# Rows of the routed tokens by one-hot products in every expert turn

## What is computed

```python
def _hier_moe(u, p, l):
    g_idx = jnp.argmax(g_logits, axis=-1)                  # one group of 4
    top_v, top_i = lax.top_k(e_in, TOP_K)                  # 2 experts of its 4
    w = jax.nn.softmax(top_v, axis=-1) * p_group[..., None]
    ...
    hg = jnp.einsum('bld,edf->blef', u, p['moe_w_gate'][l])
    hu = jnp.einsum('bld,edf->blef', u, p['moe_w_up'][l])
    h = jax.nn.silu(hg) * hu * gates.astype(u.dtype)[..., None]
    return jnp.einsum('blef,efd->bld', h, p['moe_w_down'][l])
```

## Time and profile before

| | us |
|---|---|
| median of 3 runs (1232.44 to 1235.7) | 1234.98 |
| the profiled execution | 1224.85 |
| its span | 1223.0 |
| TensorE busy, matmuls | 1114.9 (91%) |
| TensorE busy, weight loads (beside the matmuls) | 622.1 (51%) |
| VectorE busy | 389.9 (32%) |
| ScalarE busy | 233.9 (19%) |
| POOL busy | 140.8 (12%) |

### The profile page before, as it was taken

How to read it: one execution, slowest core, us unless ns; L and a number is a source line. 1 busy time by engine, 2 the same in 40 slices (tenths; PEclk the granted TensorE clock), 3 DMA queues, 4 the chain that set the end, 5 groups by cost and what they waited for, 6 DMA issues and landing times.

```text
span 1223.0 us, 23538 instructions
## 1 busy us (share of the span) xinstructions
PE 1114.9 (91%) x10201; PEld 622.1 (51%) x10201; DVE 389.9 (32%) x1023; ACT 233.9 (19%) x501; POOL 140.8 (12%) x163
## 2 busy tenths in 40 slices
PE   5899999899989959988889999999998995998986
PEld 3443445555575535545455555545666553555543
DVE  3201331574251300111233633587624230101104
ACT  2002201321231111101053232321012111111112
POOL 1043100022120000000010000042232000000001
PEclk9999999999989989999999999999998998999998
DMA  9998755359559998999996202002395999899994
GB/s 385 398 304 288 312 206 209 145 174 406 200 233 336 405 386 331 371 395 417 416 324 209 73 16 69 1 1 69 153 360 218 367 407 383 324 374 398 406 419 176
DMA packets 73018, 338.24 MB, mean 277 GB/s; under 512 B 6740, under 2 KB 16243, under 8 KB 58128
## 3 DMA queue, kind: packets, MB, share of 16 engines
q1 hardware_dynamic: 60760, 299.14, 63.2%
q0 software_dynamic: 10864, 36.42, 8.6%
q10 hardware_dynamic: 1288, 1.14, 0.3%
HBM read 314.24 MB, written 22.44 MB: 275 GB/s over the span
## 4 chain that ended last, share of the span: by engine, by line
PE 68%; DMA 18%; DVE 7%; issue 2%; ACT 2%; SPq 1%; POOL 1%; ACTq 0%; DVEq 0%; POOLq 0%
PE ps L2359 16%; DMA ring<-in_moe_w_up 12%; PE ps L1987 11%; PE ps L2562 10%; PE ps L2065 8%; PE ps L2383 7%; PE ps L2622 3%; DMA ring<-in_rec_w_in 3%; PE ps L2008 2%; PE ps L2292 2%; PE ps L2592 1%; PE ps L2342 1%; PE ps L2369 1%; PE ps L1980 1%; ACT work L1183 1%
## 5 line engine op out<-in xcount | busy, mean ns | idle before, releaser
L2359 PE MATMUL ps<-ring,work 128*32 128x256 f32 x4736 | 295.8, 394 | 53.4 <-DMA ring<-in_moe_w_up 49.3
L2359 PEld LDWEIGHTS ps<-ring,work 128*32 128x32 f32 x4736 | 150.4, 113 | 152.4 <-issue 66.3
L2562 PE MATMUL ps<-uT,ring 128*128 128x386 f32 x384 | 128.8, 488 | 0.9 <-issue 0.9
L2383 PE MATMUL ps<-ring,work 128*32 128x256 f32 x1728 | 103.0, 380 | 2.1 <-DVE work L1814 2.1
L2562 PEld LDWEIGHTS ps<-uT,ring 128*128 128x128 f32 x384 | 71.7, 190 | 49.6 <-issue 2.4
L1814 DVE COPY work<-ps 128x128 f32<-128x128 f32 x74 | 21.5, 291 | 235.4 <-PE ps L2369 234.3
L2065 PE MATMUL ps<-uT,ring 128*128 128x384 f32 x256 | 89.2, 505 | 3.0 <-DMA ring<-in_rec_w_in 1.9
L1195 ACT ACTIVATE work<-ps 128x128 f32<-128x128 f32 x74 | 20.5, 277 | 337.0 <-PE ps L2359 337.0
L1987 PE MATMUL ps<-ring,uT 128*128 128x512 f32 x192 | 84.1, 595 | 0.0
L2383 PEld LDWEIGHTS ps<-ring,work 128*32 128x32 f32 x1728 | 55.8, 110 | 39.8 <-DVE work L1814 3.0
L1810 DVE TENSOR_TENSOR work<-ps,work 128x128 f32<-128x128 f32 x74 | 21.6, 292 | 155.6 <-ACT work L1195 155.6
(11 more groups left out here) (371 smaller groups left out, 1194.9 us busy)
## 6 DMA issues: line engine op xcount, KB each, us to landing
ring<-in_moe_w_gate SPq DMA_DIRECT2D x32, 2048.0 KB, 12.8
ring<-in_moe_w_up SPq DMA_DIRECT2D x32, 2048.0 KB, 18.0
ring<-in_ada_w SPq DMA_DIRECT2D x24, 2048.0 KB, 11.3
ring<-in_moe_w_down SPq DMA_DIRECT2D x22, 2048.0 KB, 24.1
uT<-in_moe_w_down SPq DMA_DIRECT2D x10, 1536.0 KB, 16.4
ring<-in_rec_w_in SPq DMA_DIRECT2D x6, 2048.0 KB, 23.5
ring<-in_hy_w_in SPq DMA_DIRECT2D x6, 2048.0 KB, 13.4
y_rows<-work SPq DMA_DIRECT2D x64, 96.0 KB, 12.7
```

Source lines behind the costliest of these rows:

```text
L2359: ins = pe.matmul(bank(key)[32 * q:32 * q + 32, 0:2 * P].rearrange("p (a n) -> p a n", a=2), xg[:, u, k, 32 * i:32 * i + 32], ring[:, 3 * ...
L2383: ins = pe.matmul(bank(key)[32 * q:32 * q + 32, 0:256], hT[:, (FIRST[p] + i) % 2, 32 * k:32 * k + 32], w[:, q * 256:(q + 1) * 256], start= ...
L2562: ins = pe.matmul(bank(key)[:, 0:T + 2], w[:, k, (m % 4) * P:(m % 4 + 1) * P], uH[:, k, :], start=(k == 0), stop=(k == DC - 1))
```

## The change

The rows of all turns are now gathered as turn 0's were. `rows_t(p, h)` is 12 products a half (4 feature blocks by 3 token blocks) with the token rows as weights and `oh0[:, j, 0:n]` as what streams, n being 96, 64 or 32, where there were four transposes. It waits for the turn's table (`first_slots`). `fixed_slots` builds the tables of turns 0 to 2, `ranked_slots` those of the ranked turns, from the slot numbers that VectorE has: two small subtractions, three comparisons and three that compare and add. There is one buffer `oh0`, so each waits for the products of the turn before. POOL does not scatter or load rows any more; it stores the three blocks of `utok` to `x_rows` once, for the overflow path, which loads them back from there in plain order if it is taken. The clearing of `x_rows` is gone, and so is SyncE's wait for the rows. POOL's gather of results waits for the last turn's products, since it overwrites `utok`.

```diff
@@ SyncE, step(p)
                     full(sp, (l, p, "GU", TILES[p] - 1))
-                    if p == 0:
-                        sp.wait_ge(S("rows1_loaded"), 16 * (l * (NE // 2) + 1))
-                        sp.wait_ge(S("rows0_loaded"), 16 * (l * (NE // 2 - 1) + 1))
                     load_part(0, e, u)
@@ POOL
-            for a0, p_, n in ((0, P, ROWS // P), (ROWS // P * P, ROWS % P, 1)):
-                pool.dma_start(x_dram[a0:a0 + p_ * n, :].rearrange("(p a) (h n) -> p (a h) n", p=p_, n=512),
-                               bc(zeros[0:p_].unsqueeze(1), [p_, 2 * n, 512])).then_inc(S("x_rows_cleared"), 16)
...
-                pool.wait_ge(S("rows_known"), l + 1)
-                if l == 0:
-                    pool.wait_ge(S("x_rows_cleared"), 32)
                 for n, j in enumerate(BY_ROWS):
                     pool.wait_ge(S("u_rows"), NT * l + n + 1)
-                    for q in range(2):
-                        pool.indirect_dma_start(x_dram, bass.IndirectOffsetOnAxis(ap=ridx[:, j, q:q + 1], axis=0),
-                                                utok[:, j, :], None).then_inc(S("x_rows_stored"), 16)
-                pool.wait_ge(S("x_rows_stored"), 16 * 2 * NT * (l + 1))
-
-                for p in range(1, NE):
-                    u, n = p % 2, CAPS[p]
-                    if p >= 2:
-                        full(pool, (l, p - 2, "X", 1))
-                    pool.dma_start(ug[0:n, u, :], x_dram[BASES[p]:BASES[p] + n, :]).then_inc(S(f"rows{u}_loaded"), 16)
-
+                    pool.dma_start(x_dram[j * P:(j + 1) * P, :], utok[:, j, :]).then_inc(S("row_tables"), 16)
                 pool.wait_ge(S("picks_known"), l + 1)
                 for u in range(2):
                     pool.wait_ge(S(f"y{u}_stored"), 4 * 16 * STORED * (l + 1))
+                full(pool, (l, NE - 1, "X", 1))
@@ VectorE
-                for j in range(NT):
-                    ins = v.tensor_scalar(oh0[:, j, :], iota[:, 0:CAP], pl[:, j, 0:1], mask[:, j, 0:1], ALU.is_equal, ALU.mult)
-                ins.then_inc(S("first_slots"), 1)
+
+                def fixed_slots(p):
+                    if p:
+                        full(v, (l, p - 1, "X", 1))
+                    for j in range(NT):
+                        ins = v.tensor_scalar(oh0[:, j, :], iota[:, 0:CAP], pl[:, j, p:p + 1], mask[:, j, p:p + 1], ALU.is_equal, ALU.mult)
+                    ins.then_inc(S("first_slots"), 1)
+
+                def ranked_slots(p):
+                    n, local = CAPS[p], [R5[q][:, :, 0] for q in range(2)]
+                    full(v, (l, p - 1, "X", 1))
+                    v.tensor_scalar(local[0], R1[7], -float(BASES[p]), None, ALU.add)
+                    chain(v.tensor_scalar(local[1], R1[8], -float(BASES[p]), None, ALU.add))
+                    for j in range(NT):
+                        ins = v.tensor_scalar(oh0[:, j, 0:n], iota[:, 0:n], local[0][:, j:j + 1], None, ALU.is_equal)
+                    chain(ins)
+                    for j in range(NT):
+                        ins = v.scalar_tensor_tensor(oh0[:, j, 0:n], iota[:, 0:n], local[1][:, j:j + 1], oh0[:, j, 0:n], ALU.is_equal, ALU.add)
+                    ins.then_inc(S("first_slots"), 1)
+
+                fixed_slots(0)
...
                 ins.then_inc(S("rows_known"), 1)
+                fixed_slots(1)
...
                 rows_in(1)
+                fixed_slots(2)
...
                             rows_in(p + 1)
+                            if p + 2 < NE:
+                                ranked_slots(p + 2)
@@ TensorE, rows_t(p, h)
-                    if h == 0:
-                        pe.wait_ge(S(f"rows{u}_loaded"), 16 * (l * (NE // 2 - 1 + u) + p // 2 + u))
+                    pe.wait_ge(S("first_slots"), NE * l + p + 1)
                     opened(pe, key)
-                    for n in range(4):
-                        k = 4 * h + n
-                        ins = pe.transpose(bank(key)[:, n * CAP:n * CAP + n_], ug[0:n_, u, k * P:(k + 1) * P], ident[0:n_, 0:n_])
+                    for n, j in enumerate(BY_ROWS):
+                        for q in range(4):
+                            k = 4 * h + q
+                            ins = pe.matmul(bank(key)[:, q * CAP:q * CAP + n_], utok[:, j, k * P:(k + 1) * P], oh0[:, j, 0:n_],
+                                            start=(n == 0 and q == 0), stop=(n == NT - 1 and q == 3))
                     done(ins, key)
```

More of the change, by code:

```diff
@@ L75, in tables @@
         np.eye(P), (i[:, None] < i[None, :]), np.tile(i, (P, 1)),
-        i[:, None] + P * np.arange(NT)[None, :], np.tile([4, 3, 2, 1], (P, 1)),
+        i[:, None] + P * np.arange(NT)[None, :] - T, np.tile([4, 3, 2, 1], (P, 1)),
         np.tile(ROWS - CAP + P * np.arange(NE), (P, 1))], axis=1).astype(np.float32)
@@ L141, in build @@
         o = 3 * P
-        tokid, w4, obase = tc_[:, o:o + NT], tc_[:, o + NT:o + NT + 4], tc_[:, o + NT + 4:o + NT + 4 + NE]
+        less, w4, obase = tc_[:, o:o + NT], tc_[:, o + NT:o + NT + 4], tc_[:, o + NT + 4:o + NT + 4 + NE]
         ones = sb("ones", [P, P])
@@ L793, in _ @@
             clear(zeros[:], "zeros_cleared")
-            clear(gkw, "gkw_cleared")
+            clear(gkw, "rec_small_cleared")
             clear(g36, "g36_cleared")
-            clear(mcol, "mcol_cleared")
+            clear(mcol, "rec_small_cleared")
             pool.memset(vb[:, :, :, DV:DV + 1], 1.0).then_inc(S("vb_ones"), 1)
@@ L945, in between @@
                                 if out:
-                                    pool.indirect_dma_start(rows, where, here_, None).then_inc(S(f"over{l}_moved"), 16)
+                                    pool.indirect_dma_start(rows, where, here_, None, bounds_check=XROWS - 1, oob_is_err=False).then_inc(S(f"over{l}_moved"), 16)
                                     pool.wait_ge(S(f"over{l}_moved"), moved - 16 * (2 * NT - 1 - 2 * j - q))
@@ L950, in between @@
                         pool.wait_ge(S(f"over{l}_moved"), moved)
-                    between(x_dram, late_from, False, FETCHED)
+                    for j in range(NT):
+                        for q in range(2):
+                            pool.dma_start(tok_rows[l][q][:, j, :], x_dram[j * P:(j + 1) * P, :]).then_inc(S(f"over{l}_moved"), 16)
+                    pool.wait_ge(S(f"over{l}_moved"), FETCHED)
                     for n in range(2 * NE * OVF):
```

9 lines of the change are left out of this document (5 added, 4 removed).

## The result

The changed kernel takes 1331.9 us (median of four runs, 1330.9 to 1333.7), the kernel before beside it 1234.6 us (1232.4 to 1235.7). The ratio is 1.0795, with a 95% interval of 1.0766 to 1.0825: 97 us slower, in the range (1300 to 1337), 11 us over the 1321 us that were forecast. The profiled execution took 1330.9 us with a span of 1329.1, against 1224.9 with a span of 1223.0: 106.1 us more.

What follows compares the result with a forecast made beforehand. TensorE was taken as the bound, with holes in the expert stages where it waits for weights. Layer terms of +45.0 and +46.9, together +92 us on 1224.85, gave 1317, or 1327 for the median; 1321 taken, range 1300 to 1337.

Steps and rivals of the forecast that it cites:

- The sum: Both layers' stages: +45.0 us in layer 0 and +46.9 in layer 1, together +92 us on the profiled 1224.85 us.
- The products: TensorE's gathers: 48 records of 0.112 us, 5.4 us each whatever the turn's size, 15 of them 80.4 us a layer.
- the rival by columns: TensorE's gathers: cost goes by streamed columns, 47 us a layer instead of 80, time 1265 us; chance 5%.
- What the holes give back: Expert stages: all TensorE waits for gate and up weights go, -25.6 us in layer 0 and -23.7 in layer 1.
- The copies that the waits had hidden: VectorE's copy of gathered rows between turns, 0.70 us, exposed in three turns a layer: +2.1 us a layer.
- VectorE: Turns 1 to 3: building one-hot tables delays the hidden-row copy that TensorE's down product needs, +6.2 us a layer.
- The memory traffic: DMA: dropped clearing, scatters and row loads, and weights asked for some 5 us sooner, change nothing but the margin.
- The clock: TensorE in the expert stages: granted clock at 1.00 from turn 1 to the end of the stage.
- The rival of the clock: Six new stalls on VectorE each bring a slow tile at the lower clock, 1.6 us each: 1331 us; chance 11%.
- The 10 us left open: Median over profiled execution before: if in waits for weights they vanish (1317 us), otherwise they stay (1327); 1321 taken.
- the transposes: TensorE's old gathers, eight transposes each, 15 a layer, removed by the change: 12.6 us a layer saved.
- the slow tiles behind them: Tiles at half clock after three of six weight waits a layer go with the waits: -5.5 us a layer.

Runs made afterwards that it cites:

- e1_wide: The changed kernel with every gather streaming all 96 columns, also in turns of 64 and 32 rows: 1316.1 us, ratio 1.0763 to the kernel before.
- e5_turn6: The kernel before with only turn 6's rows gathered by products, in both layers: 1235.0 us, ratio 0.9993 to the kernel before.
- e6_turn3: The kernel before with only turn 3's rows gathered by products, in both layers: 1249.4 us, ratio 1.0102 to the kernel before.
- e4_two_tables: The changed kernel with two buffers for the one-hot tables, built ahead of the copy of gathered rows: 1323.2 us, ratio 1.0815 to the kernel before.
- e8_both: The changed kernel with all gathers streaming 96 columns and two buffers for the one-hot tables: 1313.1 us, ratio 1.0632 to the kernel before.
- e7_late_and_clear: The changed kernel with the later request for turn 2's weights and the early clearing of the rows put back: 1332.1 us, ratio 1.0794.
- e3_no_wait: The kernel before without SyncE's wait for the rows of turns 1 and 2, nothing else changed: 1241.1 us, ratio 1.0153.
- e0_after: The changed kernel itself, run again without edits: 1333.1 us, ratio 1.0797 to the kernel before.
- e10_before: The kernel before, run again with a profile and the same code: 1236.7 us, ratio 1.0031 to the kernel before beside it.

## Why the prediction was right, and where it was off

**The sum.** The prediction went to 1317 us for the profiled execution, 1327 for the median, and took 1321. The kernel that differs by the columns and so by the clock, e1_wide, had a span of 1312.6 us, 1314.4 with what lies around it. So the forecast sum of +92 us stands against +89.6 for the change without the clock's fall, and +106.1 with it. That the first two are so near is luck in part: below, single terms are off by up to 7 us, and the errors cancel.

**The products.** Right in kind: the streamed columns do not matter, and the rival by columns falls. From its start to the start of what follows, a gather came to 5.44 us in one piece and to 5.5 to 5.7 in two halves, not 5.4 throughout. The 0.112 us per record were right inside a group, but with the step into it and the step out of it a group takes some 0.16 us more (24 x 0.112 = 2.69 us by the spacing, 2.85 measured). The 15 gathers of layer 0 came to 84.4 us at the full clock and those of layer 1 to 83.6, for 80.4: the term was 7.2 us too small over both layers. What a record pays for was not tested by itself; that it is the loading of weights is the prediction's reading.

**What the holes give back.** Right: all waits for weights are gone, in turn 6 too, and the granted clock up to 606 us is 1.00 in the profile of the result. The copies that the waits had hidden cost 2.2 us more in layer 0, as forecast, and 0.8 in layer 1 for 2.1. e5_turn6 and e6_turn3 show the rule behind it from both sides: in the hole of turn 6 a gather cost nothing that can be measured, at turn 3 it cost some 6 us a layer with its stall.

**VectorE.** Right in place, three stalls a layer in turns 1 to 3, but forecast too large: 4.3 and 5.5 us for 6.2, and of the 5.5 us 1.2 were in the kernel before. So the change added 8.6 us in both layers for 12.4. e4_two_tables and e8_both confirm that the tables are the cause.

**The memory traffic.** Right: e7_late_and_clear shows that the earlier request and the missing clearing are worth nothing together, and e3_no_wait that the wait was no loss before either.

**The clock.** This is the step that was wrong. The prediction said: granted clock 1.00 from turn 1 to the end of the stage, with a rival by which the new stalls would lower it. The clock fell mostly not at the stalls but behind the gathers of 32 columns, at the end of each stage above all, and cost 15.2 us (3.4 in layer 0's stage, 5.0 in its tail, 6.8 in layer 1's stage) by the comparison with e1_wide; the trace of e0_after gives 16.3 in the same places. Rows of the trace before could have warned of it: its eight transposes of 32 rows are 0.68 us long, the products that replace them 5.6 us, and nothing in the trace before has TensorE stream 32 columns for that long. The rival of the clock had the right size (1331 us) by the wrong cause; its 11% are no credit to it.

The Trainium skill, "TensorE: Matmul & The Clock Gate", "Back-to-back issue gap", from whose rate a gather was estimated at 3.9 us, is not borne out for this form: 0.112 us between records here, and 5.4 to 5.7 us for a gather.

**The 10 us left open.** They did not carry over: the changed kernel's profiled execution and median agree within 1 us (1330.9 and 1331.9), so the 1317 was the better base. The guess at the cause was wrong, though. A second trace of the kernel before, 8.8 us longer, shows 44.1 us of waits for weights and not 59. It shows 4.0 us more from the last gate and up product on, with a late activation and a slow tile, and the rest in small pieces. What holds ScalarE there is open.

In sum, for the profiled executions: 92 + 7.2 (gathers) + 15.2 (clock) - 3.8 (stalls, 8.6 us for 12.4) - 1.2 (copies, 3.0 for 4.2) - 2.8 (an earlier turn 0) = 106.6, and 106.1 were seen. The terms for the transposes, the vanished waits and the slow tiles behind them are taken as forecast in this. The earlier turn 0 is scatter between executions (351.6 and 354.6 us in two traces of the changed kernel) and no effect of the change. The forecast came within 0.8% of the median since two terms too small (gathers and clock) met smaller ones too large and the 4 us that were kept of the 10. The range held in spite of the clock, and only because the wrong rival had a like size.

## What to carry to other kernels

A one-hot product with 128x128 weights costs the same 0.112 us a record whether 96, 64 or 32 columns stream. So 48 records in the place of eight transposes take nearly seven times as long (5.6 us for 0.84, the mean over the turns), and that costs nothing only where TensorE has a wait to fill at that very place. Time added to the engine that releases the next load is not given back in a later hole. Where many short streams follow one another, look at the granted clock before and after them: here, streaming 96 columns of which up to 64 were not needed cost some 0.6 us a layer and gave 15 us.

## What the runs showed of the hardware

- TensorE's clock fell from 2.4 to 1.2 GHz while the engine was busy: after gathers with 32 columns the granted clock was 0.50 from 650 to 665 us, where it stayed at full level with 96 columns streamed in the same records. With 64 it stayed in layer 0 and fell in part in layer 1 (0.83 from 1280 to 1300 us). In e0_after it also fell behind turn 5's gathers of 32 columns.
- The kernel before takes 1222.9 and 1223.7 us on two chips and 1233 to 1237 on others, 1% apart, while work that TensorE bounds took 289.46 or 289.47 us in a trace from each of four chips, two of either kind (290.5 to 290.9 us in the other traces from the slower kind).
- ScalarE ran the last tile's activation of layer 1 some 2 to 5 us after it was free to in four traces of fourteen (e5_turn6, e6_turn3, e8_both, e10_before), with no releaser that the trace names; the same code ran without it in the first trace of the kernel before. It wasn't settled what holds it.
